# Stationary weights read with a step of two columns, the host interleaving the columns

## What is computed

```
for l in 0..1:                                   # first block, depth 2
    x = x + 0.5 * swiglu(rmsnorm(x))             # 1024 -> 2816 -> 1024
    x = x + mixer(rmsnorm(x))                    # conv, short conv, window attention, forgetting attention,
                                                 # each with its own gate of 1024 columns, then w_out
    x = x + 0.5 * swiglu(rmsnorm(x))
for i, kind in enumerate((diff, hgrn, sgu, diff)):   # second block, depth 4
    x = x + mixer[kind](rmsnorm(x))
    x = x + cross_attention(rmsnorm(x), memory)  # 256 memory rows
    x = x + swiglu(rmsnorm(x))
out = rmsnorm(x)
```

## Time and profile before

| | |
|---|---|
| runs | 2864.52, 2870.81, 2885.74 us |
| profiled execution, its span | 2878.8 us (the profile gives no other time for it) |
| TensorE matmuls | 24180, busy 98% |
| TensorE weight loads | 24180, busy 96% |
| GpSimd, ScalarE, VectorE | busy 73%, 46%, 37% |
| mean granted TensorE clock | 0.989 |
| HBM traffic | 490 MB read, 171 GB/s over the span |

### The profile page before, as it was taken

One profiled execution on the slowest core, in us unless ns is written; L12 is line 12 of the kernel. 1 busy time (PEld: TensorE's weight loads), 2 busy tenths in 40 slices (PEclk: granted clock), 3 DMA queues, 4 the chain that ended last, 5 costly groups with the idle time before them and its releaser, 6 DMA issues.

```text
span 2878.8 us, 55910 instructions
## 1 busy us (share of the span) xinstructions
PE 2822.3 (98%) x24180; PEld 2771.7 (96%) x24180; DVE 1066.5 (37%) x1865; ACT 1333.4 (46%) x1490; POOL 2108.9 (73%) x462
## 2 busy tenths in 40 slices
PE   8999999999999999999999999999999999999998
PEld 8999889999999899999999998999999999999998
DVE  4217534213155443445333144333123331453331
ACT  5335544344355454345443484444354443454442
POOL 6777657878876578776768783659886688767785
PEclk9999999999999899999999999999999999999999
DMA  7974344555554355554445542445554455544553
GB/s 231 193 198 170 135 144 176 191 185 188 199 184 152 112 192 189 182 185 147 168 169 191 191 177 87 158 144 197 191 204 153 147 195 196 191 147 161 176 192 116
DMA packets 74197, 496.88 MB, mean 173 GB/s; under 512 B 8399, under 2 KB 13135, under 8 KB 14968
## 3 DMA queue, kind: packets, MB, share of 16 engines
q1 hardware_dynamic: 68344, 485.88, 46.9%
q10 hardware_dynamic: 5632, 7.62, 2.7%
HBM read 490.05 MB, written 3.41 MB: 171 GB/s over the span
## 4 chain that ended last, share of the span: by engine, by line
PE 86%; POOL 4%; DMA 3%; issue 3%; DVE 2%; ACT 2%; ACTq 0%; SPq 0%; POOLq 0%; DVEq 0%
PE G L454 21%; PE G L456 21%; PE G L455 21%; PE S L454 5%; PE S L456 5%; PE S L455 5%; POOL wl L400 4%; DMA raw<-w_units 2%; PE G L691 1%; PE S L1042 1%; ACT wh L1113 1%; DMA bias<-tables 0%; PE S L842 0%; PE S L799 0%; PE S L805 0%
## 5 line engine op out<-in xcount | busy, mean ns | idle before, releaser
L400 POOL TENSOR_TENSOR wl<-raw,wh 128x2048 fp32r<-128x2048 f32 x458 | 2108.7, 4616 | 740.5 <-ACT wh L1113 719.0
L1113 ACT ACTIVATE wh<-raw 128x2048 fp32r<-128x2048 f32 x456 | 873.7, 1918 | 1045.6 <-DMA raw<-w_units 1045.5
L454 PE MATMUL G<-ah,wl 128*128 128x256 f32 x4304 | 1209.2, 281 | 15.6 <-DVE wl L1768 8.9
L455 PE MATMUL G<-al,wh 128*128 128x256 f32 x4304 | 1200.6, 279 | 0.0
L456 PE MATMUL G<-ah,wh 128*128 128x256 f32 x4304 | 1200.3, 279 | 0.0
L454 PEld LDWEIGHTS G<-ah,wl 128*128 128x128 f32 x4304 | 816.4, 190 | 24.1 <-issue 15.1
L455 PEld LDWEIGHTS G<-al,wh 128*128 128x128 f32 x4304 | 815.2, 189 | 0.6
L456 PEld LDWEIGHTS G<-ah,wh 128*128 128x128 f32 x4304 | 814.1, 189 | 0.0
L454 PE MATMUL S<-gh,wl 128*128 128x256 f32 x1408 | 391.4, 278 | 3.4 <-POOL wl L400 3.4
L455 PE MATMUL S<-gl,wh 128*128 128x256 f32 x1408 | 391.3, 278 | 0.0
L456 PE MATMUL S<-gh,wh 128*128 128x256 f32 x1408 | 391.2, 278 | 0.0
(11 more groups left out here) (371 smaller groups left out, 3786.3 us busy)
## 6 DMA issues: line engine op xcount, KB each, us to landing
raw<-w_units SPq DMA_DIRECT2D x459, 1024.0 KB, 4.8
bias<-tables ACTq DMA_DIRECT2D x24, 128.0 KB, 3.2
tables<-trow ACTq DMA_DIRECT2D x12, 192.0 KB, 9.0
con<-consts SPq DMA_DIRECT2D x1, 1056.0 KB, 16.8
x<-x_in SPq DMA_DIRECT2D x4, 256.0 KB, 5.8
raw<-w_units SPq DMA_DIRECT2D x4, 256.0 KB, 6.9
memx<-mem_in ACTq DMA_DIRECT2D x1, 1024.0 KB, 7.4
out<-full SPq DMA_DIRECT2D x4, 256.0 KB, 2.5
```

Of the source, the lines that this page charges most:

```text
L400: pool.tensor_tensor(wl[:, j * UW:(j + 1) * UW], raw[:, j * UW:(j + 1) * UW], wh[:, j * UW:(j + 1) * UW].bitcast(F32), ALU.subtract)\
L454: pe.matmul(out, sl, vh, start=start and k == 0, stop=False, **kw)
L455: pe.matmul(out, sh, vl, start=False, stop=False, **kw)
L1113: act.activation(wh[:, j * UW:(j + 1) * UW], raw[:, j * UW:(j + 1) * UW], ACT.Copy)\
```

## The change

In every product in features form the two 128-column halves of a 256-column stretch are no longer its first and its second 128 columns but its even and its odd ones: the stationary operand is read with a step of two fp32 elements (8 bytes), beginning at element 0 or 1. The host reorders the columns of each 256-column stretch so that the even places hold what was the first half and the odd places what was the second; outputs land where they did. Units in tokens form keep their order (`token_columns_of`), since there the weights are the moving operand, read in one stretch as before. The unit that is used both ways keeps it too, and its features part (`first_features`) reads 128 adjoining columns as before. The tables of instructions of all engines are the same in number, kind and order; tensors, offsets, semaphores and DMAs are unchanged.

```diff
--- before.py
+++ after.py
@@ -448,6 +448,10 @@
             def wcut(t, j, first, width):
                 return t[:, j * UW + first:j * UW + first + width]
 
+            def every_other(j, first, odd):
+
+                return tuple(wcut(t, j, first, 2 * P).rearrange("p (i f) -> p f i", f=2)[:, odd, :] for t in (wh, wl))
+
             def product(out, parts, start, stop, **kw):
 
                 for k, (sh, sl, vh, vl) in enumerate(parts):
@@ -456,16 +460,22 @@
                     ins = pe.matmul(out, sh, vh, start=False, stop=stop and k == len(parts) - 1, **kw)
                 return ins
 
-            def features(out, j, xh, xl, fcs=2, col=256, halfway=None):
-
-                for fc in range(fcs):
+            def features(out, j, xh, xl, halfway=None):
+
+                for fc in range(2):
                     if fc and halfway is not None:
                         halfway()
                     for k in range(KD):
-                        parts = [(wcut(wh, j, k * 256 + fc * P, P), wcut(wl, j, k * 256 + fc * P, P),
-                                  xh[:, k * T:(k + 1) * T], xl[:, k * T:(k + 1) * T])]
-                        ins = product(out[:, fc * col:fc * col + T], parts, k == 0, k == KD - 1)
+                        parts = [(*every_other(j, k * 256, fc), xh[:, k * T:(k + 1) * T], xl[:, k * T:(k + 1) * T])]
+                        ins = product(out[:, fc * 256:fc * 256 + T], parts, k == 0, k == KD - 1)
                 return ins
+
+            def first_features(out, j, xh, xl):
+
+                for k in range(KD):
+                    parts = [(wcut(wh, j, k * 256, P), wcut(wl, j, k * 256, P),
+                              xh[:, k * T:(k + 1) * T], xl[:, k * T:(k + 1) * T])]
+                    product(out[:, 0:T], parts, k == 0, k == KD - 1)
 
             def features_by_input(out, j, xh, xl, acts, pieces=False):
 
@@ -629,7 +638,7 @@
                     for kt in range(2):
                         for dc in range(KD):
                             out = y[dc // 4][:, (dc % 4) * T:(dc % 4 + 1) * T]
-                            parts = [(wcut(wh, j, kt * D + dc * P, P), wcut(wl, j, kt * D + dc * P, P),
+                            parts = [(*every_other(j, kt * D + dc // 2 * 256, dc % 2),
                                       gh[:, src + kt * T:src + kt * T + T],
                                       gl[:, src + kt * T:src + kt * T + T])]
                             ins = product(out, parts, first and kt == 0 and dc % 2 == 0,
@@ -731,7 +740,7 @@
                 keys, both = g_bank(copied), g_bank(copied)
                 pe.wait_ge(low_ready, unit[0] + 1)
                 j = unit[0] % RING
-                features(keys, j, ah, al, fcs=1)
+                first_features(keys, j, ah, al)
                 tokens(both, j, ah, al).then_inc(unit_done, 1)
                 unit[0] += 1
                 projection(2, copied, ah, al)
@@ -2770,6 +2779,11 @@
 
 
 
+def interleaved(a):
+
+    return a.reshape(a.shape[0], -1, 2, P).transpose(0, 1, 3, 2).reshape(a.shape)
+
+
 def column_unit(a):
 
     return a.reshape(KD, P, 256).transpose(1, 0, 2).reshape(P, UW)
@@ -2777,10 +2791,14 @@
 
 def row_unit(a):
 
-    return a.reshape(2, P, D).transpose(1, 0, 2).reshape(P, UW)
+    return interleaved(a).reshape(2, P, D).transpose(1, 0, 2).reshape(P, UW)
 
 
 def columns_of(a):
+    return [column_unit(interleaved(a[:, n:n + 256])) for n in range(0, a.shape[1], 256)]
+
+
+def token_columns_of(a):
     return [column_unit(a[:, n:n + 256]) for n in range(0, a.shape[1], 256)]
 
 
@@ -2799,7 +2817,8 @@
 
         out += columns_of(win[:, 0:1280])
         q = win[:, 1280:1536].reshape(D, 4, HD)[:, [0, 2, 1, 3]].reshape(D, 256)
-        out += [column_unit(q)] + columns_of(win[:, 1536:2560])
+        out += [column_unit(interleaved(q))] + token_columns_of(win[:, 1536:1792])
+        out += columns_of(win[:, 1792:2304]) + token_columns_of(win[:, 2304:2560])
         gates = win[:, 2564:]
         for b in BRANCHES:
             own = columns_of(gates[:, b * D:(b + 1) * D])
@@ -2808,18 +2827,20 @@
         out += columns_of(v["w_out"][l])
         out += ffn_units(v["ffn2_w_gate"][l], v["ffn2_w_up"][l], v["ffn2_w_down"][l])
     for i, kind in enumerate(MIXERS):
-        kv = columns_of(v["ca_w_kv_2"][i])
+        keys, values = v["ca_w_kv_2"][i][:, 0:D], v["ca_w_kv_2"][i][:, D:]
+        kv = columns_of(keys) + token_columns_of(values)
         if kind == "diff":
-            a = columns_of(v["da_w_in_2"][i // 3])
+            a = v["da_w_in_2"][i // 3]
+            a = columns_of(a[:, 0:2 * D]) + token_columns_of(a[:, 2 * D:])
             out += [a[n] for n in (0, 4, 8, 9, 1, 5, 10, 11, 2, 6, 3, 7)] + kv[0:4]
             out += columns_of(v["da_w_out_2"][i // 3])
         elif kind == "hgrn":
             a = v["hg_w_in_2"][i // 3]
-            out += (columns_of(a[:, D:2 * D]) + columns_of(a[:, 0:D]) + columns_of(a[:, 2 * D:]) + kv[0:4]
+            out += (columns_of(a[:, D:2 * D]) + columns_of(a[:, 0:D]) + token_columns_of(a[:, 2 * D:]) + kv[0:4]
                     + columns_of(v["hg_w_out_2"][i // 3]))
         else:
             a = v["sg_w_in_2"][i // 3]
-            out += columns_of(a[:, D:]) + columns_of(a[:, 0:D]) + kv[0:4] + columns_of(v["sg_w_out_2"][i // 3])
+            out += token_columns_of(a[:, D:]) + columns_of(a[:, 0:D]) + kv[0:4] + columns_of(v["sg_w_out_2"][i // 3])
         out += columns_of(v["ca_w_q_2"][i]) + kv[4:8] + columns_of(v["ca_w_o_2"][i])
         out += ffn_units(v["ffn_w_gu_2"][i][:, :DFF], v["ffn_w_gu_2"][i][:, DFF:], v["ffn_w_down_2"][i])
     assert len(out) == UNITS
```

## The result

The change made the kernel slower. Its median is 2969.40 us (2968.70 to 2972.09, four runs) against 2871.57 us for the kernel before; the ratio is 1.0343 with a 95% interval of 1.0311 to 1.0375.

The account below looks back on a forecast made before the run. It took TensorE's distance between matmuls, 115.0 ns on average, to bound the kernel. The step's -69 us plus 4 us lost to waits gave -65 us, from 2870.8 to 2806 us; range 2750 to 2972 us.

Parts of the forecast that it names:

- What bounds the kernel: Whole kernel: TensorE's cost per fp32r matmul with its weight load in dense streams, mean 115.0 ns; weight supply has room.
- Part 1, the step of two: 20,160 features-form loads: equal pace of both reads brings 115.0 ns to 111.6, -69 us; bounds 109 to 222 ns.
- The nearest row: Passes of fp32 matmuls, both reads advancing at equal pace: their 111.6 ns was taken as the stepped load's distance.
- Part 2, the odd halves: Features-form loads of odd columns begin 4 bytes further; taken as costing nothing.
- Parts 3 and 4: 4,020 unchanged loads keep their distance; supply by GpSimd and transfers still fits at 111.6 ns; mixer waits take back 4 us.
- The rival "bad distance": Every features product: equal-pace reads that start on each other stay so, 120.0 ns, +101 us, 2972 us; chance 0.13.
- The rival "no change": Dense stretches: something other than the two addresses sets the levels, so the step changes nothing; 2871 us; chance 0.26.
- The rival "a stepped read is a slow read": Features-form loads cover twice the bytes; if paid by bytes, 222 ns each and 5030 us; chance 0.10.
- The rule weighed: Trainium skill on TensorE: moving operand and weight load have independent read ports; by it the step gains 0, not -69 us.

## Why the prediction was wrong

- **What bounds the kernel** was right. The time moved with the distance between matmuls: 101 us by the distances, 97 us on TensorE's row, 98 us in the medians.
- **Part 1, the step of two, is where it failed.** It took equal pace of the two reads for what makes the fp32 passes cheap (111.6 ns), and carried that distance over to a stepped load. But bursts of fp32r products at step 1 show the same 111.7 with 64 moving columns, where there is no equal pace, and with 128, which is equal pace as the prediction meant it, at two places. So rows 10 give what a contiguous load costs beside few moving columns, with or without equal pace. The stepped load costs 117.8 ns by itself, and with 256 moving columns beside it 120.0. The term was -69 us; it is +101.
- **The nearest row was near in the wrong quantity.** The fp32 passes were alike in pace, yet their stationary reads were contiguous, and the step was the thing changed. The bounds of the part did reach past 120 (109 to 222 ns), so "no row shows it" deserved more weight than the likeness.
- **Part 2, the odd halves**: right for this kernel, even and odd both 120.0 at places 0 and 192. A begin 8 bytes into a 16-byte stretch, which the change never has, costs 2.2 ns beside 64 or 128 moving columns and nothing beside 256.
- **Parts 3 and 4**: the distances of unchanged reads (tokens products 115.9 against 116.4 ns) and the supply were as said; what GpSimd and the transfers would have done at 111.6 ns was not tested by the change itself.
- **The rival "bad distance"** gave the right time, 2972 us, from 120.0 ns of L934. Its mechanism did not hold: step 2 takes about 120 at all 16 places, and the kernel does not get faster at the one other place tried. What it had right is that contiguous reads at equal places take 120 ns. That the stepped ones take the same 120.0 is luck as far as the runs show, and the range reached 2969 us only through this rival.
- **The rival "no change"** expected that something else than the addresses picks the level. For contiguous reads that is half right: at 192 bytes the same operands show both levels. But the place moves them too, and the stepped products stand at 120.0.
- **The rival "a stepped read is a slow read"** was the true mechanism for more than half of the cost, with the wrong price. The load is not paid by bytes read at today's distance (222 ns) but by 16-byte stretches, 1.8 ns each; by this price some 61 of them would fit under the 111.7 ns of a contiguous load (an estimate, 111.7/1.82). At step 2 the 64 stretches just stick out; at step 4 the load takes 233 ns, near what the rival feared for step 2.
- **The rule weighed.** The trace spoke against independent reads, and the runs agree: contiguous reads beside 256 moving columns take 113.3 to 120.0 ns as the places are changed. The other rule put the slow stepped read out. It is that of the Trainium skill, "Advanced Engine Details and Errata", section "SBUF Cachelines": at least two hits on a 16-byte line for full rate. Measured, two hits a line are 6.1 ns slower than four for fp32r weight loads (117.8 against 111.7), and one hit a line doubles the load (233.3).

## What to carry to other kernels

Where weight loads and matmuls are both near the limit of TensorE, a change of a load's access pattern is to be priced by the load alone, with few moving columns beside it, before the two together are reasoned about. Rows that are alike in speed but not in access pattern do not price it. Read fp32 stationary operands contiguously: here a step of two cost 3.4% of the kernel, and in the streams a step of four doubled each load. Where the operands lie is worth a trial too: with contiguous reads, equal places cost 3.6% and the best places tried gained 0.66%.

## What the runs showed of the hardware

- Beside 64 or 128 moving columns, a weight load of 128 fp32r columns is held at 111.7 ns when contiguous and at about 1.82 ns for each 16-byte stretch when that is more: 117.8, 173.3 and 233.3 ns at steps 2, 3 and 4.
- Contiguous fp32r loads beside 256 moving columns take 113.3 to 120.0 ns, by the distance between the two operands modulo 256 bytes and by the stationary one's beginning modulo 32. At 192 bytes both 113.3 and 117.8 occur; at 112 bytes with a begin on 32, only 113.3 in all twelve streams of this kind. Why these places, and what picks the level at 192, stays open.
- A stepped load and a bad place do not add up: 2978 us for the place alone, 2969 for the step alone, 2979 for both.
- In streams of 96 products with 64 moving columns the granted clock fell from 1.00 to 0.50, 2.4 to 1.2 GHz, though within a stream TensorE began a matmul every 213 to 234 ns without a gap. Contiguous loads and those at step 2 then took 213.3 ns, and loads at step 4 233.3, the same as at the full clock.
